# Index projection moved ahead of context's keys and values, with filler products at the start

## The reference

```
x = x + 0.5 * swiglu(rms_norm(x, ffn1_norm), gate, up, down)
h = rms_norm(x, mix_norm);  proj = h @ w_in
q, k, v, qi, ki, wi, u = split(proj)          # 512, 512, 512, 256, 64, 4, 512 columns
qi, ki = rope(qi), rope(ki)                   # on the first 32 of 64 dimensions
score = sum over 4 heads of wi * relu(qi . ki)     # the index; causal
idx = top_k(score, 128)                       # per query, which keys attention may see
attn = softmax over the chosen keys (8 heads);  pooled = multiscale_pool(u) @ pool_w
x = x + concat(attn, pooled) @ w_out;  x = x + 0.5 * swiglu(...)
```

```
h_c = ctx * (1 + scale_c) + shift_c           # 256 context tokens
k_a, v_a, k_b, v_b = h_c @ w_in_2[...] + b_in_2[...]     # 4 x 128 columns
k_b = rms_norm(k_b) * k_norm_g                # per head of 64
```

## Time and profile before

| | us |
|---|---|
| median of 3 runs | 1738.71 (1737.01 to 1739.12) |
| the profiled execution | 1738.32 |
| its span in the trace | 1736.5 |
| PE busy in it | 1705.2 (98%) |
| DVE, POOL, ACT busy | 977.5, 930.2, 665.8 |

### The profile page before, as it was taken

One profiled execution on the slowest core, in us unless ns is written; L12 is line 12 of the kernel. 1 busy time (PEld: TensorE's weight loads), 2 busy tenths in 40 slices (PEclk: granted clock), 3 DMA queues, 4 the chain that ended last, 5 costly groups with the idle time before them and its releaser, 6 DMA issues.

```text
span 1736.5 us, 24431 instructions
## 1 busy us (share of the span) xinstructions
PE 1705.2 (98%) x8123; PEld 1388.1 (80%) x8123; DVE 977.5 (56%) x1507; ACT 665.8 (38%) x1382; POOL 930.2 (54%) x755
## 2 busy tenths in 40 slices
PE   8999999999999999999999999999999999999997
PEld 7888888888777888888888888864478988888887
DVE  4258645768985467352123529578767673542544
ACT  5322222343466433223223323665632642332333
POOL 4554453567982445544444545467943755544541
PEclk9999999999999999999999999999999999999998
DMA  7354452534211346523423433100122234333321
GB/s 236 109 179 148 146 158 85 176 93 133 73 49 49 122 146 189 150 86 98 126 83 86 122 97 89 33 1 25 49 61 85 71 93 140 97 97 98 97 85 49
DMA packets 279967, 178.39 MB, mean 103 GB/s; under 512 B 6537, under 2 KB 258629, under 8 KB 279749
## 3 DMA queue, kind: packets, MB, share of 16 engines
q1 hardware_dynamic: 265620, 149.36, 29.9%
q10 hardware_dynamic: 14256, 27.87, 4.7%
HBM read 175.11 MB, written 2.10 MB: 102 GB/s over the span
## 4 chain that ended last, share of the span: by engine, by line
PE 91%; DVE 5%; ACT 1%; issue 1%; DMA 1%; POOL 1%; SPq 0%; DVEq 0%; ACTq 0%; POOLq 0%
PE ps L973 89%; DVE mod_acc L2345 2%; PE ps L1455 1%; DVE stat L2662 0%; DVE ps L2688 0%; PE ps L1280 0%; DMA mod_raw<-in_w_mod 0%; DMA xnat<-in_x 0%; POOL wL L806 0%; PE ps L1660 0%; ACT prob2B L2091 0%; POOL actL L860 0%; DVE x L2388 0%; PE ps L1405 0%; PE ps L1154 0%
## 5 line engine op out<-in xcount | busy, mean ns | idle before, releaser
L806 POOL TENSOR_TENSOR wL<-raw,wH 128x512 fp32r<-128x512 f32 (+2 forms) x560 | 747.4, 1358 | 709.1 <-ACT wH L1768 698.1
L973 PE MATMUL ps<-actH,wH 128*128 128x512 f32 (+1 forms) x1312 | 510.6, 389 | 2.6 <-POOL actL L860 1.9
L973 PE MATMUL ps<-actH,wL 128*128 128x512 f32 (+1 forms) x1312 | 503.6, 384 | 0.0
L973 PE MATMUL ps<-actL,wH 128*128 128x512 f32 (+1 forms) x1248 | 480.0, 385 | 0.0
L1768 ACT ACTIVATE wH<-raw 128x512 fp32r<-128x512 f32 (+2 forms) x558 | 311.1, 608 | 295.5 <-PE ps L973 295.4
L973 PEld LDWEIGHTS ps<-actH,wH 128*128 128x128 f32 x1312 | 247.1, 188 | 53.5 <-issue 2.4
L973 PEld LDWEIGHTS ps<-actH,wL 128*128 128x128 f32 x1312 | 246.4, 188 | 49.1
L973 PEld LDWEIGHTS ps<-actL,wH 128*128 128x128 f32 x1248 | 235.1, 188 | 46.7 <-DVE actL L2310 0.8
L973 PE MATMUL ps<-hidH,wH 128*128 128x512 f32 (+1 forms) x720 | 267.6, 372 | 0.0
L973 PE MATMUL ps<-hidH,wL 128*128 128x512 f32 (+1 forms) x720 | 266.6, 370 | 0.0
L973 PE MATMUL ps<-hidL,wH 128*128 128x512 f32 (+1 forms) x720 | 266.5, 370 | 0.0
(11 more groups left out here) (378 smaller groups left out, 2039.8 us busy)
## 6 DMA issues: line engine op xcount, KB each, us to landing
mod_raw<-in_w_mod ACTq DMA_DIRECT2D x24, 1024.0 KB, 6.1
raw<-in_w_in SPq DMA_DIRECT2D x48, 512.0 KB, 3.7
raw<-in_ffn_w_up SPq DMA_DIRECT2D x44, 512.0 KB, 3.8
raw<-in_w_up SPq DMA_DIRECT2D x44, 512.0 KB, 3.9
raw<-in_ffn_w_gate SPq DMA_DIRECT2D x43, 512.0 KB, 3.8
raw<-in_ffn_w_down SPq DMA_DIRECT2D x32, 512.0 KB, 4.0
raw<-in_w_out SPq DMA_DIRECT2D x16, 512.0 KB, 3.8
raw<-in_w_down SPq DMA_DIRECT2D x16, 512.0 KB, 3.8
```

Of the source, the lines that this page charges most:

```text
L806: nc.gpsimd.tensor_tensor(wL[:, b:b + w // 2], raw[:, b:b + w // 2], wH[:, b:b + w // 2].bitcast(F32), ALU.subtract).then_inc(lo_ready, 1)
L973: return nc.tensor.matmul(out, a, b, start=first, stop=last)
```

## The change

Stage `idx` stands ahead of `ctxkv` in the order of weights, and on PE, ACT and POOL. `idx` now waits for each tile of actL by itself (`tiles=KT`), so that it can begin behind `f1_down2`. `row_sums(1)` moves into `idx`, and its results to bank 3. On DVE the bias of the context's keys and values comes behind the rotation of `pi`, and the norm of k_b behind the first attention. PE turns `pi` behind slab 0 of `pool` rather than slab 1, and scores from step 13 (`SCORES_FROM`) rather than 20. All rounds for the tile with 384 keys now come before `k_scale`; of tile 3's 16 rounds, 11 come before the attention's loop and 5 in it (units 5, 7, 9, 13, 17), where there were 6 and 10. At the start `awake` has PE multiply `ones` by `ones` (128x128, results unused): 6 products as soon as `ones` is there, and one behind each of the first three pieces of x.

```diff
@@ weights
 ffn("f1", ...)
+rows("idx", w_in, 3 * ATT, IDX_COLS, 2)
 stage("ctxkv", 4, SLAB, ...)
-rows("idx", w_in, 3 * ATT, IDX_COLS, 2)
@@ tables
+SCORES_FROM = 13
-PICK_AT = range(2, 22, 2)
+PICK_AT = (5, 7, 9, 13, 17)
@@ gpsimd
-if st["name"] == "idx":
-    pool.wait_ge(slab_done, stage_of["ctxkv"]["base"])
+if st["name"] == "ctxkv":
+    pool.wait_ge(slab_done, stage_of["idx"]["base"])
@@ tensor
+def awake(n):
+    for _ in range(n):
+        product(bank(3, P), ones[:], ones[:], True, True)
+
+pe.wait_ge(cleared, 2)
+awake(6)
 pe.wait_ge(const_in, 16)
...
         x_block(k, q)
+    awake(1)
...
+def before_idx():
+    pe.wait_ge(mod_cols, 7)
+def idx_sums(j):
+    if j == 2:
+        row_sums(1, 3)
+token_tiles("idx", IDX_COLS, 4, before_idx, tiles=KT, inside=idx_sums)
 (ctxkv)
-    if (j, kk) == (2, 2):
-        row_sums(1)
+    if k == 0 and b == 3:
+        pe.wait_ge(rn_ready, 2)
-def before_idx():
-    pe.wait_ge(act_ready, 2 * KT)
-    pe.wait_ge(rn_ready, 2)
-    pe.wait_ge(mod_cols, 7)
-token_tiles("idx", IDX_COLS, 4, before_idx)
 (pool)
-    if j * KT + k >= 2 * KT + 4:
-        idx_score(j * KT + k - (2 * KT + 4))
+    if 0 <= j * KT + k - SCORES_FROM < (ST - 1) * IDX_HEADS:
+        idx_score(j * KT + k - SCORES_FROM)
 if j == 0:
     spread_rows(1, 7)
-if j == 1:
     idx_turns()
@@ scalar
-slabs("ctxkv", 0, nothing)
 token_stage("idx", 4, pi, IDX_COLS)
+slabs("ctxkv", 0, nothing)
@@ vector
-row_scale(1, RMS_EPS)
+row_scale(1, RMS_EPS, 3)
-(bias of ctxkv, norm of k_b, sink)
 gained_tables(cv("cos1"), cv("sin1"), gain1, 1, DH // 2)
 (rotation of pi)
+(bias of ctxkv)
 rows_spread(1, 7)
...
 pick(1)
-pick(2, 0, 11)
+pick(2)
+pick(3, 0, 2)
 head_scales(1, 0, k_scale[:], (k_scaled, 1))
-pick(2, 11)
-pick(3, 0, 2)
+pick(3, 2, 7)
 (rotation and scale of q's first two tiles)
-pick(3, 2, 5)
+pick(3, 7, 10)
...
 first_attention()
 (last of attn's lows)
+(norm of k_b, sink)
 last_down("out1", ...)
```

More of the change, by code:

```diff
@@ L979, in split_product, with row_sums @@
             return product(out, wl, xh, False, last)
-        def row_sums(n):
+        def row_sums(n, b=4):
             pe.wait_ge(acc_done, ACC_TOTAL[n])
             for q in range(ST):
-                mm = product(ps[:, 4, q:q + 1], acc[:, q * P:(q + 1) * P], ones[:, 0:1], True, True)
+                mm = product(ps[:, b, q:q + 1], acc[:, q * P:(q + 1) * P], ones[:, 0:1], True, True)
             mm.then_inc(row_sum, 1)
@@ L1914, in _ @@
         for j in range(SLOTS):
-            if j == 3:
-                relus(4, 12)
+            relus(*(min(max(KT * n - SCORES_FROM, 0), (ST - 1) * IDX_HEADS) for n in (j, j + 1)))
             act.wait_ge(slab_done, stage_of["pool"]["base"] + j + 1)
@@ L1919, in _ @@
             split(stage_of["k"], 0, j)
-            if j == 1:
+            if j == 0:
                 act.wait_ge(idx_T, 1)
@@ L1923, in _ @@
                     nc.scalar.activation(kiT[half, :], ps[0:DH, 6, :], ACT.Copy).then_inc(idx_keys, 1)
-                relus(0, 4)
         token_stage("k", 4, k1, ATT, wait=(idx_rel_used, 12))
@@ L2279, in rsqrt, with row_scale, row_root @@
                     link(ins)
-        def row_scale(n, eps):
+        def row_scale(n, eps, b=4):
             dve.wait_ge(row_sum, n)
[L2284 to L2288, removed]
+            link(V.tensor_scalar(small[:, 0:ST], bank(b, ST), eps, None, ALU.add))
+            row_root(n, b)
+        def row_root(n, b=4):
+            rsqrt(rn[:], small[:, 0:ST], ST, last=(rn_ready, n + 1), room=bank(b, ST, 64) if n else None)
         def rows_spread(n, b=5):
@@ L2532, in _ @@
         link(V.tensor_scalar(wi, wi, IDX_SCALE, None, ALU.mult))
+        kc = kctx[:].rearrange("p (q v b d) -> p q v b d", q=CT, v=NKV, b=2)
+        for g, v in ((0, vA), (1, vB)):
+            dve.wait_ge(slab_done, stage_of["ctxkv"]["base"] + 2 * g + 2)
+            for q in range(CT):
+                b = 2 * g + q
+                link(V.tensor_tensor(kc[:, q, :, g, :], bank(b, P).rearrange("p (v d) -> p v d", d=DH),
+                                     biasx[:, g * 256:g * 256 + P].rearrange("p (v d) -> p v d", d=DH), ALU.add))
+                V.tensor_tensor(v[:, q * P:(q + 1) * P], bank(b, P, P), biasx[:, g * 256 + P:g * 256 + 256],
+                                ALU.add).then_inc(drained_v, 1)
         rows_spread(1, 7)
@@ L2596, in during1 @@
             if n in PICK_AT:
-                pick(3, 6 + PICK_AT.index(n), 7 + PICK_AT.index(n))
+                pick(3, 11 + PICK_AT.index(n), 12 + PICK_AT.index(n))
         def rest_of_v(n):
             if n == 1:
-                pick(3, 5, 6)
+                pick(3, 10, 11)
                 for q, (done, count) in ((1, (v_block, 2)), (3, (slab_done, stage_of["v"]["base"] + SLOTS))):
@@ L2733, in _ @@
             V.tensor_tensor(tile(hidL, k), bank(AT1_BANK[k]), tile(hidH, k).bitcast(F32), ALU.subtract).then_inc(hid_ready, 1)
+        dve.wait_ge(drained_v, drain_base["ctxkv"] + 4)
+        kb = kctx[:].rearrange("p (n b d) -> p n b d", b=2, d=DH)[:, :, 1, :]
+        tk = tA[:, 0:2 * P].rearrange("p (n d) -> p n d", d=DH)
+        link(V.tensor_tensor(tk, kb, kb, ALU.mult))
+        link(V.tensor_reduce(small[:, 0:4], tk, AX_X, ALU.add))
+        link(V.tensor_scalar(small[:, 0:4], small[:, 0:4], 1.0 / DH, QK_EPS, ALU.mult, ALU.add))
+        rsqrt(small[:, 128:132], small[:, 0:4], 4)
+        link(V.tensor_tensor(kb, kb, small[:, 128:132].unsqueeze(2).broadcast_to([P, 4, DH]), ALU.mult))
+        V.tensor_tensor(kb, kb, gain2[:, DH:].unsqueeze(1).broadcast_to([P, 4, DH]), ALU.mult).then_inc(kctx_ready, 2)
+        dve.wait_ge(kctx_ready, 2)
+        link(V.tensor_scalar(sink[:, NH:], sink[:, 0:NH], -1.0, None, ALU.mult))
         last_down("out1", 1.0, "ffn2_norm", 2 * KT, 2 * KT, 2 * KT, ACC_TOTAL[1])
```

## The result

| | before | after |
|---|---|---|
| median, us | 1738.49 (1735.45 to 1739.12, 6 runs) | 1745.08 (1744.37 to 1745.95, 6 runs) |
| profiled execution | 1738.32 | 1744.96 |
| its span | 1736.5 | 1743.1 |

The ratio is 1.0037, 95% interval 1.0027 to 1.0047: the change makes the kernel slower by 0.37%, which is little but clear of the noise. Forecast was 1744.8.

What follows compares the result with a forecast made beforehand. PE was taken to bound the kernel (91% of the chain that ended last). Terms 1 to 4 summed as 1738.3 + 7.0 + 1.7 - 2.0 - 0.2 = 1744.8 us; range over the cases 1734.5 to 1749.

Steps and rivals of the forecast that it cites:

- Term 1: Ahead of `pool` slab 0: PE waits while POOL's lows hold DVE's rotation of `pi`; cost 7.0 us, bounds 0.9 to 15.
- Term 2: Just behind the wait ahead of `pool`: PE's clock falls to half speed; cost 1.7 us, bounds 0 to 3.4.
- Term 3: Search starts 4.9 us earlier relative to PE, five rounds leave the attention; gain 2.0 us, bounds 0 to 4.5.
- Term 4: Filler products, with first products spaced 0.23 rather than 0.42; gain 0.2 us, between -0.9 and 1.3.
- Hidden: Norm of k_b, 11.6 us of DVE, moved before `out1`'s evictions, where DVE waits for PE anyway: costs nothing.
- The faster one: Rival: POOL leaves gaps, rotation keeps its old rate, 0.9 us wait, no clock loss; 1733.9 us, chance 0.24.
- The short wait: Rival case of a short wait, chance 0.13; the text given has no further details or time for it.
- The search is late: Rival: more rounds ahead of `k_scale` and q's rotation make PE wait at `v` and q's turn; 1748 us, chance 0.07.

Runs made afterwards that it cites:

- e1: Changed kernel with the four bias instructions that empty banks 0 and 1 moved between the rotation of `pi`'s second and third tiles; 1737.13 us, ratio 0.9992.
- e2: Changed kernel with POOL's lows of `ctxkv` and `pool` in four instructions of 256 columns per slab instead of two of 512; 1739.10 us, ratio 1.0004.
- e3: Changed kernel with the rotation of `pi` in 4 instructions over all four tiles instead of 16, same elements; 1736.19 us, ratio 0.9985.
- e4: Changed kernel with 24 products of `ones` by `ones`, results unused, on PE ahead of its wait for bank 0 before `pool`; 1742.04 us, ratio 1.0023.
- e5: Changed kernel with turn of `pi`, scores and search rounds put back where the kernel before has them; 1745.12 us, ratio 1.0037.
- e10: e3 with turn of `pi`, scores and search rounds where the kernel before has them; 1737.21 us, ratio 0.9999.
- e9: Kernel before, its order of stages and search kept, plus filler products at the start and the rotation of `pi` in 4 instructions; 1738.20 us, ratio 1.0004.
- e7: e3 with `pi` turned ahead of `pool`'s slab 0, scores from step 9, 13 of tile 3's rounds before the attention's loop; 1738.00 us, ratio 0.9996.
- e6: Changed kernel without the nine filler products of `ones` at the start; 1745.55 us, ratio 1.0040.
- e8: e3 repeated unchanged with more rounds of measurement; 1736.79 us against 1738.02 for the kernel before, ratio 0.9997.

## Why the prediction was right

**Term 1, forecast 7.0, measured 5.9.** The mechanism was right: ten lows, each holding one rotation instruction. The bank was empty 1.2 us earlier than forecast for two reasons. The tables were done at 397.36, not 398.3, so three rotation instructions went ahead of the lows, not one, and three were left behind them, not five. And the lows ended at 411.20, not about 412: they began 0.3 earlier and took 12.90, ten times 1.29, without the 0.4 of DVE's own time that the sum put between them. (The 4.7 given for the 16 instructions without POOL leaves out the gaps between them: an unheld tile took 1.27 in before, 412.94 to 414.21, so 5.1.) e1, e2 and e3 each take another link out (the order, the length of the lows, the number of DVE's instructions), and the wait goes, shrinks to the 2.14 that 0.74 an instruction leaves, and goes.

**Term 2, forecast 1.7, measured 2.35.** The half clock lasted 4.70 us of PE's work, not 3.4, and with the 2.1 of it that fell in the wait about 6.8: twice the stretch in the attention from which the term was taken. e4 shows that it is a thing of its own: the wait stays, the loss (2.3 by the traces) goes.

**Term 3, forecast a gain of 2.0, measured 2.75, but made up otherwise.** 1.33 is the stretch at half clock, counted at 0.5, and it is not a gain: it turned up at 1200 instead. 0.67 is the search's own, by e5 (0.66) and e10 (0.69), where 1.5 was counted. 0.73 came from q's rotation, which no longer met a low of POOL. The prediction held that place for a draw; it had no term for what an earlier end of `pi`'s rotation does to POOL, by way of `rB`. e9 shows it in the old order too (0.72 between 487 and 512 us), and e7, where POOL is late again, loses part of it. So the gain that stays is 1.42, not 2.0. The count of waits named in the profile falls by only 0.8 while the attention is 1.42 shorter without the clock; where the other 0.6 stand stays open.

**Term 4, forecast 0.2, measured 0.27 by 380 us.** The 0.2 and its bounds, -0.9 and 1.3, were the author's estimate; no run shows what they were drawn from, and the agreement is luck. What the runs showed in its place is a pace that differs: the six fillers from 1.48 on took 2.93 us together, the one at 5.21 took 0.22, and products at full pace began 1.3 sooner (14.64 against 15.95), the whole upper bound. 1.0 of it was lost again by 33 us; PE waits there 0.8 for a DMA (`vec_rows<-in_conv_w`). The sum had no such wait. How much the fillers give differs from execution to execution: at 40 us nine of the ten traces with them are 0.1 to 1.0 ahead of before, and e9 is 1.8 behind; e6, without them, is 0.3 behind. So the range given (-0.9 to 1.3) was too narrow below.

**Hidden, forecast nothing, measured nothing:** behind the moved norm of k_b the changed kernel is 5.26 behind at 600 us and 5.28 at 700.

**Not foreseen:** the 1.33 us at half clock in the second attention. It undoes the clock's share of term 3: before has one such stretch in its attentions, and so has the changed kernel. In the trace the whole loss is 6.64, where 6.5 was forecast, but the parts were off by more: 1.1 too much for term 1, 0.65 too little for term 2, and a lasting gain in term 3 that was 0.6 smaller than counted. That these cancel to 0.1 is luck; the sign and the size of the loss, terms 1 and 2, are not.

**The rivals.** The faster one (1733.9) fell with the 1.3 us rotation instructions. The short wait (chance 0.13) did not come here; e2 made one: 2.14 us of wait, no half clock, 1739.10. "The search is late": the search began at 446.82, 438.8 in before's clock (forecast 438.5), `k_scale` was ready ahead of PE, and there was no wait at `v`.

**A better version?** The order of the change with the rotation in 4 instructions was the fastest, 1736.19 and 1736.79 in two sets against 1738.64 and 1738.02, but only the first interval (0.9975 to 0.9994) excludes that nothing changed; the second (0.9988 to 1.0006) does not. That it beats the kernel before is likely and not shown.

## What to carry to other kernels

Before an instruction that empties a bank is moved behind others on DVE, count those that POOL holds (with two inputs in SBUF, and TENSOR_SCALARs in SBUF) while it works without gaps, and give each the length of a POOL instruction, not its own (here 1.3 us instead of 0.33, and 1.15 instead of 0.17 for the TENSOR_SCALAR of e3). Where that bites, fewer and longer instructions on DVE shorten it (14.9 to 5.8 us in e3, at 1.2 us more for two lows of POOL), and so do shorter ones on POOL (e2, whose ten lows' worth took 14.53 instead of 12.90). Look also at what waits behind the moved work: here an earlier copy let POOL run over 2 us ahead, which paid 0.73 us, 70 us later. A PE wait behind full load costs its own length and may cost half clock behind it as well (5.94 and 2.35 us here, 2.14 and nothing in e2); and a difference of 1.3 to 1.6 us between two traces may be one stretch of half clock that stands elsewhere in the other, so compare offsets stage by stage before giving it to an edit.

## What the runs showed of the hardware

- A DVE instruction of two SBUF inputs beside POOL's took about 1.3 us with lows of 512 columns and 0.7 with lows of 256, whether it had 80 columns or 160 of its own; with PSUM as one input it took 0.29 beside lows of 512 (e1).
- A TENSOR_SCALAR with one input, in SBUF, was held too: the scale of `wi` took 0.17 beside an idle POOL (changed kernel), 0.58 beside lows of 256 (e2), 1.15 beside lows of 512 (e3). The search's MAX8 was not: 0.56 each time beside six lows in a row (before, 464.5 to 471.3).
- Holding goes both ways: beside DVE instructions of 640 columns POOL's low took 1.88 instead of 1.3 (e3).
- In a wait of 5.94 us the clock fell to half, 3.8 us into it; in one of 5.75 us (e6) it fell 2.0 us into it, at 410.8. In one of 2.14 us (e2) it didn't (1.00 from 407 to 420), nor in one filled with products of unused results (e4, 1.00 from 400 to 420). How long a wait may be is not shown.
- Stretches of 3.4 us at half clock, 1.3 to 1.6 us each in cost, came in the two attentions, where PE waits briefly and often (before, 507.60 to 529.20: busy 17.28 of 21.60 us): at 525.7 in before, 1199.6 in the changed kernel, 1159.5 in e1, 1160.2 in e3, 529.8 in e4, 1200.8 in e5, 1168.5 in e6, 1160.8 in e7, 1191.5 in e8, two in e9 (514.3 and 527.9) and in e10 (524.5 and 1193.5), none in e2. Equal work with equal waits had one or had none. What decides that was not found.
